# A two-layer mixer trunk on one core: inputs and output laid out by feature outside the program, and the first two tiles of a layer computed side by side

## What is computed

```python
h = rms_norm(x, ln_g)                       # mean of squares over the 1024 features
u = jnp.einsum('bsd,de->bse', h, w_in)      # one wide projection: q, k, v, z of four branches, gates
o_sb, o_fx, o_dl = stick-breaking, forgetting and dilated-window attention over x
mkv = jnp.einsum('bmd,de->bme', rms_norm(mem, mem_ln_g), w_mem_kv)   # 256 memory tokens
o_mm = attention of q_mm over mkv
y_b = einsum(o_b * silu(z_b), w_br_b)       # for each branch b
merged = sum over b of sigmoid(gate_b) * y_b
return x + jnp.einsum('bsd,de->bse', merged, w_out)
```

## Time and profile before

| | |
|---|---|
| median of 3 runs | 1245.41 us (1244.69 to 1245.96) |
| the profiled execution: time | 1244.55 us |
| its span in the trace | 1242.8 us |
| PE busy | 1223.4 us, 98% of the span |
| ACT, DVE, POOL busy | 681.3, 633.5, 684.8 us |
| DMA | 120.83 MB, 97 GB/s on average |

### The profile page before, as it was taken

The page is one execution under the profiler, slowest core; times in us unless marked ns, Lnnn a source line. Parts: engine busy times, 40 slices in busy tenths (PEclk is TensorE's granted clock), DMA queues, the critical chain, the costliest instruction groups (busy, mean ns, idle before and its releaser), DMA issues.

```text
span 1242.8 us, 18333 instructions
## 1 busy us (share of the span) xinstructions
PE 1223.4 (98%) x6378; PEld 992.0 (80%) x6378; DVE 633.5 (51%) x1125; ACT 681.3 (55%) x1301; POOL 684.8 (55%) x563
## 2 busy tenths in 40 slices
PE   7999999999999999999999999999999999999998
PEld 6888888777777888887888888887777788888876
DVE  6788533876745222223349874357676442222221
ACT  6775544776554544544458744357755454544531
POOL 3675523574343676776457664237634346776762
PEclk9999999999999999999999999999999999999999
DMA  7654422222222344443365443122222224444342
GB/s 225 171 134 127 102 52 59 60 69 69 65 56 68 98 115 103 106 114 111 102 168 148 126 119 85 44 55 74 60 69 60 60 73 118 102 115 102 103 119 85
DMA packets 209891, 120.83 MB, mean 97 GB/s; under 512 B 9736, under 2 KB 200328, under 8 KB 209800
## 3 DMA queue, kind: packets, MB, share of 16 engines
q1 hardware_dynamic: 209800, 119.66, 37.0%
HBM read 107.04 MB, written 6.29 MB: 91 GB/s over the span
## 4 chain that ended last, share of the span: by engine, by line
PE 92%; DVE 3%; ACT 2%; POOL 1%; issue 1%; DMA 0%; SPq 0%; DVEq 0%; ACTq 0%; POOLq 0%
PE dense L842 76%; PE score L842 6%; PE out L842 4%; PE acc L842 3%; PE acc L1149 1%; PE turn L842 1%; POOL w_lo L1816 1%; POOL dk_lo L1879 1%; PE turn L1000 0%; DMA sig<-in_x 0%; ACT w_hi L1266 0%; PE acc L1000 0%; PE score L953 0%; ACT h_hi L1233 0%; DVE o_norm L1580 0%
## 5 line engine op out<-in xcount | busy, mean ns | idle before, releaser
L1816 POOL TENSOR_TENSOR w_lo<-w_raw,w_hi 128x512 fp32r<-128x512 f32 (+1 forms) x400 | 498.2, 1252 | 519.2 <-ACT w_hi L1266 461.1
L842 PE MATMUL dense<-h_hi,w_hi 128*128 128x512 f32 (+1 forms) x1176 | 473.1, 402 | 2.6 <-DVE h_lo L1457 1.8
L842 PE MATMUL dense<-h_lo,w_hi 128*128 128x512 f32 (+1 forms) x1176 | 457.1, 389 | 0.0
L842 PE MATMUL dense<-h_hi,w_lo 128*128 128x512 f32 (+1 forms) x1160 | 450.9, 389 | 0.0
L842 PEld LDWEIGHTS dense<-h_hi,w_hi 128*128 128x128 f32 x1176 | 221.0, 188 | 59.1 <-issue 11.2
L1266 ACT ACTIVATE w_hi<-w_raw 128x512 fp32r<-128x512 f32 (+1 forms) x401 | 231.6, 585 | 66.2 <-PE dense L842 65.9
L842 PEld LDWEIGHTS dense<-h_hi,w_lo 128*128 128x128 f32 x1160 | 217.7, 188 | 46.7
L842 PEld LDWEIGHTS dense<-h_lo,w_hi 128*128 128x128 f32 x1176 | 221.3, 188 | 39.6 <-issue 0.2
L1552 DVE TENSOR_TENSOR sig<-dense,x_rstd_row 128x512 f32<-128x512 f32 x48 | 33.2, 692 | 215.0 <-issue 122.7
L1326 ACT ACTIVATE sig<-sig 128x512 f32<-128x512 f32 x48 | 30.4, 633 | 127.9 <-DVE sig L1552 127.9
L1554 DVE TENSOR_TENSOR raw<-dense,x_rstd_row 128x512 f32<-128x512 f32 x80 | 54.8, 685 | 29.3 <-issue 18.4
(11 more groups left out here) (297 smaller groups left out, 2030.2 us busy)
## 6 DMA issues: line engine op xcount, KB each, us to landing
w_raw<-in_w_in SPq DMA_DIRECT2D x292, 256.0 KB, 2.9
w_raw<-in_w_out SPq DMA_DIRECT2D x32, 256.0 KB, 2.8
x_scratch<-v_dil SPq DMA_DIRECT2D x16, 256.0 KB, 3.5
w_raw<-in_w_mem_kv SPq DMA_DIRECT2D x16, 256.0 KB, 3.0
v_dil<-x_scratch SPq DMA_DIRECT2D x16, 256.0 KB, 2.8
turned<-normed SPq DMA_DIRECT2D x48, 64.0 KB, 2.5
inv_den<-o_norm SPq DMA_DIRECT2D x48, 64.0 KB, 2.6
silu_z<-in_mem SPq DMA_DIRECT2D x4, 512.0 KB
```

The lines of the kernel that those rows point to most:

```text
L842: return nc.tensor.matmul(o, lhsT, rhs, start=start, stop=stop, skip_group_check=True)
L1816: pool.tensor_tensor(w_lo[:, g % SPLIT_SLOTS, c], w_raw[:, g % RAW_SLOTS, c], f(w_hi[:, g % SPLIT_SLOTS, c]), ALU.subtract).then_inc(w_lo_ ...
```

## The change

1. **Layout outside.** x and mem are given to the program feature by feature (`features_apart`), the result comes back so. The 32 transposes at the start, the 16 of mem in each layer and the 32 at the end go, with their copies.
2. **Start.** SP loads weight item 0, then the eight blocks of x straight into `xT`, with items 1 to 3 among them. ACT makes h_hi block by block (512 tokens) and squares of each block, DVE makes h_lo and adds the squares (`first_add`), as layer 2 does it. `x_sum` is then one product for 512 columns.
3. **First two tiles together.** `new_together` and `together`: q0 and k0 of a layer get their weights as q0 first half, k0 first half, q0 second half, k0 second half, and the matmuls go block 0 for q0, block 0 for k0, block 1 for q0, and so on. `x_sum` stands after block 6 of both (before: after block 4 of q0 in layer 2).
4. **Memory.** Squares of mem on ACT, three additions on POOL (`mem_square`, `mem_rest`), a product with ones on PE (`mem_sum`, into T), and a row of reciprocal norms that DVE multiplies in when it moves the mk and mv tiles out. High and low parts come straight from the loaded block.
5. **Places.** Two more `room()` steps after the first pair of `col` steps and two after the second `rd` in the attention parts.
6. **End of the gated sum.** The addition of y (MM, 7) goes from POOL to DVE.
7. **Output.** The o tiles are stored as they are ready; the last one is added and stored in two halves of 256 tokens.
8. In layer 1, x is not saved to scratch and comes back from the input; the memsets of ones in v_tok and v_mem go, and these tiles lose their middle column block.

```diff
+    def new_together(*names):
+        group = [Tile(*name) for name in names]
+        for t in group:
+            t.n = len(tiles)
+            tiles.append(t)
+        for half in zip(*map(source, group)):
+            for t, s in zip(group, half):
+                t.items.append(len(stream))
+                stream.append(s)
+        return group
...
-        order = [(t, h, i) for t in group for h, item in enumerate(t.items) for i in range(source_tiles(item))]
+        order = [(t, h, i) for h in range(2) for i in range(HALF) for t in together]
+        order += [(t, h, i) for t in group if t not in together for h, item in enumerate(t.items) for i in range(source_tiles(item))]
...
-                if waiting[2] and waiting[2][-1].normed:
-                    add("low", waiting[2][-1])
+                for r in waiting[2]:
+                    if r.normed and ("low", r) not in steps[-200:]:
+                        add("low", r)
...
-    dense(named(("q", 0), ("k", 0), ("q", 2), ("k", 2), ("q", 4), ("k", 4), ("q", 1), ("k", 1)),
-          [room(), [("x_sum",)]] + [room()] * 6 + [[("mem_square",)]] + [room()] * 2 + [[("mem_scale",)]] + [room()], lag=2)
+    first = new_together(("q", DIL, 0), ("k", DIL, 0))
+    dense(first + named(("q", 2), ("k", 2), ("q", 4), ("k", 4), ("q", 1), ("k", 1)),
+          [room()] * 3 + [[("x_sum",)]] + [room()] * 2 + [[("mem_square",)]] + [room()] * 2 + [[("mem_rest",)]] + [room()] * 2 + [[("mem_sum",)]] + [room()], lag=2, together=first)
...
+            load_item(0)
+            for kt in range(KT):
+                sp.dma_start(xT[:, kt, :], x_in[:, kt, :]).then_inc(x_loaded[kt], 16)
+                if kt == 0:
                     for l in range(DEPTH):
                         sp.dma_start(ln_all[:, l * KT:(l + 1) * KT], ln_gain[l, :, :]).then_inc(params_in, 16)
+                if kt % 2 == 0 and kt < 6:
+                    load_item(kt // 2 + 1)
...
+                    elif kind == "mem_sum":
+                        wait(pe, turn_ring.before("mem_sum"))
+                        pe.wait_ge(*mem_added.of(3))
+                        for i in range(2):
+                            last = mm(T[:, 0:MEM], ones, sig[:, 0, i * MEM:(i + 1) * MEM], start=i == 0, stop=i == 1)
+                        last.then_inc(mem_total.sem, 1)
...
             act.preload_act_table_set("natural_log_exp_and_others")
-            first_square(0)
-            first_square(1)
             first_split(0)
             act.wait_ge(params_in, 16 * DEPTH)
             first_high(0)
             first_split(1)
             first_high(1)
-            first_square(2)
-            first_split(2)
-            first_square(3)
+            first_square(0)
+            first_high(2)
+            for kt in range(3, KT):
+                first_square(kt - 2)
+                first_high(kt)
+                if kt in (3, 4):
+                    first_split(kt - 1)
+            first_square(KT - 2)
+            first_square(KT - 1)
...
+            for kt in range(KT):
+                first_low(kt)
+                if kt >= 3:
+                    first_add(kt - 2)
+            first_add(KT - 2)
+            first_add(KT - 1)
...
+                            if t.branch == MM and t.idx == KT - 1:
+                                a = acc[t.idx % 2][:, :]
+                                dve.wait_ge(*y_gated.of(t.n))
+                                dve.wait_ge(*y_added.before(t.n))
+                                dve.tensor_tensor(a, a, gated[gated_ring.slot(t.n)], ALU.add).then_inc(y_added.sem, 1)
...
+                            if (l, t.idx) == (DEPTH - 1, KT - 1):
+                                for i in range(2):
+                                    c = slice(i * MEM, (i + 1) * MEM)
+                                    dve.tensor_tensor(xT[:, t.idx, c], bank_[:, c], xT[:, t.idx, c], ALU.add).then_inc(x_last, 1)
+                                continue
```

310 lines of the change are left out of this document (101 added, 209 removed).

## The result

The change makes the kernel slower: 1256.53 us (median of 4 runs, 1255.16 to 1257.12) where the kernel before takes 1245.07 (4 runs, 1244.69 to 1245.96) in the same comparison, a ratio of 1.009 with a 95% interval of 1.0078 to 1.0102. The prediction was 1236.8. The profiled execution takes 1256.8 us, its span 1254.9, 12.2 more than the earlier trace rows show.

A forecast was written before the change was run, and what follows sets the result against it. PE was taken to bound the kernel, busy 1223.4 of 1242.8 us. Terms (a) to (h) sum to -8.5 us, giving 1236.8 us; own range 1234.5 to 1239.2, for 8 in 10 1231.5 to 1241.3.

The forecast's parts named there:

- (c): Memory part, both layers: transposes -3.7, mem_sum product +1.9, PE's wait for ACT's read of T +2.1; sum +0.3 us.
- (f): Added rooms in attention, two layers: wait at first col pair -1.35, at worst 0; second place -0.6, between 0 and -1.1.
- The rival of the lower clock: Program start: PE stays at its lower clock level on dense matmuls, kernel slower by over 0.2%; chance 0.03.
- (a): Start of layer 1: q2's first matmul at 24.9 instead of 27.51, a gain of 2.6 us.
- (b): Start of layer 2: q2 starts at about 637.9 instead of 635.80, a loss of 2.1 us, bounds 1.4 to 2.5.
- a case for which the prediction said 5: Start of layer 1: DVE and POOL don't collide, constants take about 2, q2 at 22 to 23, gain 5 us.
- (d): Output transposes taken off PE: 1.75 us for the first 16, 1.3 for the other 12, so -3.05 us.
- (e): Tail after the last dense matmul: 4.35 us instead of 6.7, a gain of 2.35, from 1.9 to 2.9.
- (g): Addition of y (MM, 7) moved to DVE: -0.5 us a layer, -1.0 in all, bounds -1.5 and +1.
- (h): Rest: scratch stores, reload, memsets and narrower v tiles touch no engine PE waits for, 0 us.

The follow-up runs named there:

- e13: e10 with the squares of mem, their three POOL additions and mem_sum moved earlier, right behind x_sum: 1240.1 us.
- e17: The best version with DVE's mem_low replaced by a product with zero of one operand, leaving out the low part of mem: 1236.1 us.
- the best version: e13 with one room step after the first col pair instead of none: 1238.8 us, 0.995 of the kernel before.
- e3: The changed kernel without the two room steps after the first pair of col: 1250.5 us.
- e10: Changed kernel with mem_sum into a score bank, constants and item 6's split moved at the start, x_sum early in layer 2, no rooms after first col pair: 1242.5 us.
- e12: The changed kernel with the addition of y (MM, 7) on POOL again: 1257.9 us.

## Why the prediction was wrong

The sum was -8.5 and the span grew by 12.2. Of the 20.7 between them the memory part has 11.2, the attention part 7.6, the two starts 3.6; the output and the gated sum came out 1.7 better. One of the prediction's own signs of being wrong is there, an attention part that grows by over 2 us (5.6), and the wait at `mem_sum` was to be 1 us and is 3.8.

**(c), the step that failed.** Two of its sentences did. The first: "The squares, scalings and splits of mem move between ACT, DVE and POOL and are hidden by the 5.4 us that each tile gives them": DVE had no such time. In the windows of the kernel before (busy us of PE, PEld, DVE, ACT, POOL, then the clock, DMA share, GB/s):

```profile
39.00:45.00 6.00, 6.00 (x29) 4.95 (x28) 5.41 (x6) 4.10 (x8) 3.82 (x3) 1.00 0.65 177
45.00:51.00 6.00, 6.00 (x28) 4.99 (x27) 5.53 (x6) 5.84 (x13) 4.56 (x3) 1.00 0.60 171
51.00:57.00 6.00, 6.00 (x29) 4.95 (x28) 5.93 (x6) 3.98 (x7) 4.79 (x3) 1.00 0.59 163
57.00:63.00 6.00, 6.00 (x28) 4.99 (x27) 5.92 (x7) 5.83 (x9) 3.72 (x3) 1.00 0.52 130
```

The change made DVE slower still, twice: three more additions on POOL, beside which DVE's operations last 1.78 us instead of 0.7, and `mem_low` from SBUF instead of a PSUM bank. Moving the additions ahead, with the squares and `mem_sum`, is worth 1.3 and 1.5 us in the two layers (e13); `mem_low` with one operand gives 0.5 and 1.0 in the memory stages (e17).

The other is "PE waits 1.05 us": it took ACT's 3.3 us to T over from the earlier trace rows, while ACT's read stands behind a move by DVE; it was 6.2, and PE waited 3.8 for the 1.05 said. Shown: short additions or an earlier place take the wait down (to 1.37 and 2.67; to none). A bank of its own only spreads the same lateness over four other waits. Its upper bound, "if POOL's three additions of 1.35 make the rotation of the tiles before later, 2 a layer", named the mechanism and had the wait at half its size. The 3.7 us of transposes were not gained even in the best version: its memory stages cost 2.9 and 4.1 where the PE work alone would give -0.9. That DVE with POOL sets the pace of these tiles, so that PE's work saved turns into waits, fits the trace, but no run shows it; this part (2.9 us in each layer of e13, against -0.9) stays open.

**(f).** The wait at `col` went as said, and the second pair of rooms gave 1.0 where 0.6 was forecast. What failed is "at worst 0": the two empty steps stretch one list, so every attention step of that group falls elsewhere among the matmuls, and 130 us on a tile's `dq_lo` came ahead of the addition that the last `sb_pv` needs. That cost 2.93 us a layer and a slow stretch; e3 shows it. With one room the attention stages come out at 2.2 for the 1.95 forecast, though layer 2 pays 1.1 of that in its memory stage, and why it does is open.

**The rival of the lower clock.** I asked only how long the program's start would be slow, and gave slower 0.03. The start cost nothing, as the sum had it: PE begins at 6.44, its matmuls come every 0.43 us until 12.0 and every 0.23 behind that, and it then waits 1.55 for the squares all the same. But the clock falls again behind later waits, and a stretch costs up to 1.7 or 3.4 us of PE's time, so that a wait of 3 can be worth nearly 5. With up to 10 us for that, (c) at its upper bound (+1.9) and the two new waits of (f) (2.93 + 0.16 each), the sum of -8.5 becomes +9.6 at most, an estimate from these rows; +12.2 came.

**(a) and (b).** The mechanism was right, both times. The last square was added at 21.2, at the late bound, where 19.5 was taken. POOL's part came out as priced (DVE's operations at 11.61 and 13.31 took 1.78, together 2.1 more than alone); what the sum had not is a wait for a DMA:

```profile
7.26 0.63 ACT L1164 ACTIVATE w_hi<-w_raw 128x512 fp32r<-128x512 f32 x1 [1.84 <-DMA w_raw<-in_w_in]
```

ACT waited 1.84 us for weight item 1, and DVE behind it stood idle for 2.38. The constants took the 4.6 us; q2 was 1.6 late, and the slow stretch behind its wait took 1.5 more. (b) predicted an idle stretch of 2.1 and got 2.15, and 0.5 us more around it. A start of -2.7 is there in e10, but with the constants and the split out of the way, a case for which the prediction said 5; that it is near the -2.6 of the sum is chance.

**(d), (e), (g), (h).** The transposes of the output: from the first matmul of o0's last block to PE's last dense matmul it was 41.8 us (1193.91 to 1235.70) and is 38.7 (1212.75 to 1251.42), 3.1 less for 3.05. The tail: 3.1 us for 4.35; the last store (half a tile, 128 KB) took 2.2 us where it was priced at 3.4. The gain is 3.6 for 2.35, beyond its bound of 2.9. (g): 0.69 a layer for 0.5, shown by e12. (h): nothing found.

## What to carry to other kernels

Before work is called hidden, read how busy the engine is that hides it, in that stretch, and whether its neighbours will slow it: where DVE is busy for over 90%, an addition on POOL is not free. An empty step or a moved step in an evenly spread list moves everything behind it; look at the order at its far end too. And price a wait of PE as long as those behind which the clock fell here (2.15 us and more) with a slow stretch behind it, or fill it.

## What the hardware showed

**The clock.** Over the 20 traces, PE's waits of more than 1 us behind the first 10 us, and how many had a half-speed stretch that began in them or within 2 us behind: up to 1.8 us, 0 of 17; 2.15 us, 2 of 10; 2.39, 2 of 2; 2.6 to 2.7, 9 of 12; 2.93, 18 of 22; 3 us and more, 28 of 28. After the first 10 us none began elsewhere but at the program's end. These 59 stretches last 3.4 us, nine of them 6.8, with PE busy for all or most of it, which is up to 1.7 or 3.4 us lost. The Trainium skill, TensorE: Matmul & The Clock Gate, Part 1, has an idle PE return to 1.2 GHz too; these traces agree, and show it behind shorter waits than that page lets one expect, down to 2.15 us; the measurement decides.

**DVE beside POOL.** The same operation of `mem_low` lasts 0.47 us each of 16 times with one operand in PSUM and one in SBUF (POOL was at work all through 12 of them), 1.5 us in 11 of 16 with both in SBUF, and with a single SBUF operand 1.38 in 8 of 16, else 0.28. The prediction took from the Trainium skill, GPSIMD Engine Reference, Specifications, only the two SBUF inputs; the page also names DVE's two-port mode, and the single operand agrees with that, though no trace shows the mode itself.
